# One copy of an expert group's TensorE code per width, in a loop of seven turns

## The reference, cut to what matters

```python
D_MODEL = 1024; SEQ = 512; D_FF = 3584; N_EXPERTS = 8; TOP_K = 2

def swiglu(h, w1, w3, w2):
    return (jax.nn.silu(h @ w1) * (h @ w3)) @ w2

def moe_swiglu(h, router, w1, w3, w2):
    logits = h @ router
    top_val, top_idx = lax.top_k(logits, TOP_K)
    gates = jax.nn.softmax(top_val, axis=-1)
    ...   # tokens of each expert are collected: 1024 assignments over 8 experts
    # each expert e: yb = swiglu(xb, w1[e], w3[e], w2[e]), times its gate, added back to its tokens
```

## Time and profile before

| what | value |
|---|---|
| median of three runs | 3055.92 us |
| span of the profiled execution | 3053.4 us (its own time is not listed apart; 2.5 us below the median) |
| TensorE matmuls busy | 2671.7 us, 87% of the span, x16732 |
| VectorE, ScalarE, GpSimd busy | 32%, 20%, 8% |
| granted TensorE clock, mean | 0.914 |
| instruction fetches (DMA queue 8) | 204 packets, 3.34 MB |

### The profile page before, as it was taken

How to read it: one execution, slowest core, us unless ns; L and a number is a source line. 1 busy time by engine, 2 the same in 40 slices (tenths; PEclk the granted TensorE clock), 3 DMA queues, 4 the chain that set the end, 5 groups by cost and what they waited for, 6 DMA issues and landing times.

```text
span 3053.4 us, 43393 instructions
## 1 busy us (share of the span) xinstructions
PE 2671.7 (87%) x16732; PEld 2423.9 (79%) x16733; DVE 992.2 (32%) x1450; ACT 606.4 (20%) x873; POOL 246.2 (8%) x109
## 2 busy tenths in 40 slices
PE   7988899999989888797798995996999799697795
PEld 5776688887767767796798894995999699697794
DVE  5767333333367672221211221112111211211213
ACT  3326222222233251111011110111000111111111
POOL 4221301001042211000000000000000000000000
PEclk9879899999988788898899997997999899898897
DMA  4310232222113102384475682781555267386481
GB/s 146 91 56 21 104 96 89 96 95 91 39 57 91 60 17 83 120 295 167 151 253 178 218 292 73 266 268 58 195 195 180 78 228 233 113 296 215 170 293 65
DMA packets 135244, 445.19 MB, mean 146 GB/s; under 512 B 26448, under 2 KB 26448, under 8 KB 134992
## 3 DMA queue, kind: packets, MB, share of 16 engines
q1 hardware_dynamic: 135024, 441.72, 43.0%
HBM read 436.28 MB, written 4.19 MB: 144 GB/s over the span
## 4 chain that ended last, share of the span: by engine, by line
PE 78%; DVE 10%; issue 9%; ACT 2%; POOL 1%; DMA 0%; SPq 0%; DVEq 0%; ACTq 0%; POOLq 0%
PE pair L566 30%; PE pair L574 15%; PE pair L394 5%; PE pair L390 5%; PE pair L391 5%; PE pair L673 2%; PE pair L715 2%; PE pair L624 2%; PE pair L619 1%; PE pair L503 1%; PE pair L620 1%; PE pair L377 1%; PE pair L462 1%; DVE scr L1213 1%; PE pair L438 1%
## 5 line engine op out<-in xcount | busy, mean ns | idle before, releaser
L566 PE MATMUL pair<-xe,raw_m 128*128 128x128 f32 (+4 forms) x5376 | 702.7, 293 | 62.3 <-issue 60.9
L566 PEld LDWEIGHTS pair<-xe,raw_m 128*128 128x128 f32 x5376 | 696.2, 194 | 65.4 <-issue 65.3
L574 PE MATMUL pair<-scr 128*128 128x128 f32 (+4 forms) x3584 | 461.6, 290 | 0.0
L574 PEld LDWEIGHTS pair<-scr 128*128 128x128 f32 x3584 | 456.1, 191 | 0.0
L390 PE MATMUL pair<-xh,wh 128*128 128x512 f32 x960 | 394.3, 411 | 33.7 <-DVE xl L1054 21.7
L391 PE MATMUL pair<-xl,wh 128*128 128x512 f32 x960 | 385.8, 402 | 0.0
L1490 DVE TENSOR_TENSOR scr<-scr,pair 128x256 f32<-128x256 f32 x224 | 94.3, 421 | 819.3 <-PE pair L566 819.3
L390 PEld LDWEIGHTS pair<-xh,wh 128*128 128x128 f32 x960 | 186.5, 194 | 96.6 <-issue 24.4
L1386 DVE TENSOR_TENSOR scr<-scr,pair 128x512 f32<-128x512 f32 x224 | 154.1, 688 | 313.3 <-PE pair L574 313.3
L394 PE MATMUL pair<-xh,wl 128*128 128x512 f32 x960 | 243.3, 397 | 0.0
L566 PE MATMUL pair<-xe,scr 128*128 128x128 f32 (+4 forms) x1792 | 235.4, 290 | 0.0
(11 more groups left out here) (268 smaller groups left out, 2244.0 us busy)
## 6 DMA issues: line engine op xcount, KB each, us to landing
raw_m<-in_we SPq DMA_DIRECT2D x336, 512.0 KB, 4.2
scr<-in_we SPq DMA_DIRECT2D x336, 512.0 KB, 4.3
raw_m<-in_wmix SPq DMA_DIRECT2D x64, 512.0 KB, 4.3
raw_m<-in_wa SPq DMA_DIRECT2D x42, 512.0 KB, 3.5
scr<-in_wa SPq DMA_DIRECT2D x42, 512.0 KB, 3.5
h<-in_x SPq DMA_DIRECT2D x8, 256.0 KB, 4.3
out<-scr SPq DMA_DIRECT2D x8, 256.0 KB, 2.1
u_dram<-scr SPq DMA_DIRECT2D x2, 512.0 KB, 2.8
```

The source lines that it names most:

```text
L566: i = mm(bank[2 * (j % 2) + w][:, 0:W], raw(i_)[:, kk * P:(kk + 1) * P], xe[:, kk, 0:W], start=(kk == 0), stop=(kk == DK - 1))
L574: i = mm(ybank[q_ % 2][:, m, 0:W], raw(2 * GJ + q_)[:, (m * GJ + j) * P:(m * GJ + j + 1) * P], g[:, j, 0:W], start=(j == 0), stop=(j == GJ ...
```

## The change

TensorE's seven groups of an expert become a loop of seven turns with one group in its body. `expert_group` is unchanged, and so are the order and number of its products and waits.

```diff
             def groups(e, W):
-                with pe.Fori(0, NG // 2) as gi:
-                    for half in range(2):
-                        expert_group(e * NG + gi * 2 + NG + half, W, e)
-                expert_group(e * NG + 2 * NG - 1, W, e)
+                with pe.Fori(0, NG) as gi:
+                    expert_group(e * NG + gi + NG, W, e)
```

## The result

The kernel after takes 3069.98 us (median of six runs, 3067.2 to 3072.93), the kernel before beside it 3059.93 us (six runs, 3054.45 to 3062.87). The ratio is 1.0035, with a 95% interval of 1.0023 to 1.0046: slower by 10 us, where 3053 and no change was forecast; the forecast's own range ended at 3062, its wider one at 3064. (The 3055.92 us from which the forecast started is the median of the first three of the six runs of before.) The profiled execution of after took 3067.2 us with a span of 3065.4.

The account below looks back on a forecast made before the run. It took TensorE to be bound by matmuls, plus waits for code at jumps in the expert stage. Terms 0 + 0 - 3 + 0 = -3 us gave a 3050.4 us span and a 3053 us median, range 3045 to 3062.

Parts of the forecast that it names:

- What bounds the stage: Expert stage: TensorE's unexplained waits are fetches of code not on the engine, about 5.8 us for each such jump.
- Back edges: Ends of the group loop's turns: 32 more taken branches, covered by TensorE's queued products, priced at 0 us.
- Code not fetched in sequence: Group code of an expert: one copy run instead of three, 204 code packets becoming about 179, worth 0 us.
- Jumps: Ways into and out of the groups: same number, shorter; only the second expert's way in gains, -3 us.
- Code behind: rows, gather and scatter after the groups: moved by 50 whole packets, places nearly kept, 0 us within -6 to +6.
- The third rival: Code after the groups moves into worse places, more gather and rows jumps miss: about +20 us, 3073 us, chance 0.07.

Follow-up runs that it names:

- the kernel of seven copies: Kernel after with its loop unrolled into seven straight groups, plus 192 never-executed instructions restoring before's places for rows, gather and scatter: 3053.36 us, ratio 1.0007 to before.
- The one-copy kernel with the code behind moved back: Kernel after plus 224 never-executed instructions behind the expert groups, so rows, gather and scatter stand at before's packet places: 3051.02 us, ratio 0.9998 to before.
- the kernel before with 32 places of padding: Kernel before plus 32 never-executed instructions behind the expert groups, moving rows, gather and scatter 32 places on: 3064.43 us, ratio 1.0038 to before.
- the shift by 64 places: Kernel after plus 32 never-executed instructions behind the expert groups, so rows, gather and scatter stand 64 places further on than in before: 3079.94 us, ratio 1.0092.

## Why the prediction was wrong

- **What bounds the stage** was right: code that TensorE has to wait for, about 5 us a jump. The price of 5.8 us was high; three jumps saved gave 5.06 each in one place and 3.49 in another.
- **Back edges at 0** was right, by the groups' 21.44 us with an edge between every two, and by the kernel of seven copies. The Trainium skill, "Runtime: NRT & Kernel Launch", section "Instruction fetch mechanics", says that a taken branch whose target is outside a window of two blocks stalls. By that, bodies of 400 instructions would have stalled in some layouts; no run here shows such a stall at a back edge.
- **Code not fetched in sequence** was right: 177 packets where 179 were forecast, and 204 or 177 of them make 1 and 0.9998 of the time.
- **Jumps** at -3 us was wrong in its one gain. The wait of the second expert's way in was 9.43 us instead of the 10.24 of the earlier trace rows, where 2 to 5 us less was forecast, and behind it the eight units that took 19.11 us before took 1.88 + 0.72 + 18.23 = 20.83:

```profile
1458.93 9.43 issue
1468.36 1.88 PE pair L566 x6
1470.24 0.72 issue
1470.96 18.23 PE pair L566 x122
```

TensorE starts, does six matmuls and waits again. The one-copy kernel with the code behind moved back has the same gap (0.60 us after six), so it belongs to the groups' own code, not to the code behind. I read it as the end of a packet just behind the head of this width's loop, which ate the gain; only the gap is shown, its cause is not. The ways out of width 128 did stay, as placed: 18.14, 18.36, 19.21 and 16.62 us where before had 18.93, 18.48, 17.40 and 16.24. One expert was placed wrongly: 200 is the second of its pair (192, 200), not the first. It leaves by two jumps, in 6.01 us (6.07 before), and its jump over one width is the last of its way in, 9.05 us (9.10 before). The sum had nothing for it either way.
- **Code behind** at 0 is the step that failed. The text said that the code behind moves by "16 x 800 = 12,800 instructions, which is 50 packets exactly; it keeps its places in the packets but for a few instructions per width". Those few, two a width, are 32 places in sum; they cost 10 us in after and 13 in the kernel before with 32 places of padding, by the medians. I gave the bounds as -6 to +6 us, and 32 places cost more than the upper one. The third rival had the place right (the code behind in worse places, "about +20 us", 0.07), with a price that after halves and the shift by 64 places exceeds, and with a wrong condition: it needs no paddings, rounding is enough. It counted whole jumps more that miss; at 32 places the packets in all did not become more, only the waits became longer.

How the place makes the wait longer stays open. What fits the waits is a packet's end just behind a jump's target: the jump brings its target's packet, and the sequencer reaches the next one before that has come. This is my reading of the 1.8 to 4.0 us on the four wide experts; the runs show the dependence on the place, not the order of events within one wait.

## What to carry to other kernels

Where a program chooses by its data among many copies of a stage, look for waits at the jumps between the copies, and cut their number on the likely path: put the likeliest case behind one compare (here 2.5 to 2.7%). The number of copies and the back edges of a loop cost nothing measurable here, with bodies of some 400 and 800 instructions that go round without a fetch; a longer body was not tried. An edit that only changes the length of code moves everything behind it, and here this alone moved the time by 0.2 to 0.9%; before a gain or a loss of that size is laid to an edit, pad unreached code until the rest stands where it stood.

## What the runs showed that I had not expected

The place of code alone, with the same instructions run in the same order, gave 0.9998, 1.0020, 1.0035 and 1.0092 of before's time at shifts of 0, -40, +32 and +64 instructions. And a step of 32 places acts much alike on a program of 28,700 and one of 15,900 instructions ahead of the shifted code (1.0038 and 1.0035).
